# Layer-norm rows scaled by a diagonal matmul at the stage edges of a fused two-block kernel, and bias rows loaded in six parts

## The reference

```python
# first block, per layer l (c_act = silu(c); sh, sc, gt are six vectors of width 1024)
    ada = c_act @ w_ada[l] + b_ada[l]
    u = x * (1.0 + sc1) + sh1
    y = mixer(u, ...)                      # w_in (4608 columns), attention, conv, w_out
    x = layer_norm(DN_ALPHA * x + (1.0 + gt1) * y, ln_mix_g[l], ln_mix_b[l])
    u = x * (1.0 + sc2) + sh2
    h = square(relu(u @ w_up[l])) @ w_down[l]
    x = layer_norm(DN_ALPHA * x + (1.0 + gt2) * h, ln_ffn_g[l], ln_ffn_b[l])
# second block, per layer
    proj = rmsnorm(x, ln_mix_g[l]) @ w_in[l]          # 4128 columns
    # three attentions; two add a bias per head, a function of the distance of query and key
    qc = rmsnorm(cq, mla_q_norm_g[l]) @ w_uq[l]       # its last columns are rotated (rope)
```

## Time and profile before

| | us |
|---|---|
| median of 3 runs | 1823.41 |
| the profiled execution | 1823.75 |
| its span in the trace | 1822.0 |
| PE busy | 1758.1 (96%) |
| DVE busy | 1275.3 (70%) |
| ACT busy | 890.5 (49%) |

### The profile page before, as it was taken

The page is one execution under the profiler, slowest core; times in us unless marked ns, Lnnn a source line. Parts: engine busy times, 40 slices in busy tenths (PEclk is TensorE's granted clock), DMA queues, the critical chain, the costliest instruction groups (busy, mean ns, idle before and its releaser), DMA issues.

```text
span 1822.0 us, 27283 instructions
## 1 busy us (share of the span) xinstructions
PE 1758.1 (96%) x9254; PEld 1451.1 (80%) x9254; DVE 1275.3 (70%) x1973; ACT 890.5 (49%) x1530; POOL 54.8 (3%) x111
## 2 busy tenths in 40 slices
PE   8999999998999999999999999999999999999998
PEld 3776778996766789988898877788789989778886
DVE  5788897667788885568547887555555579865555
ACT  1456334443455444444556664444445557544443
POOL 0000010000000000001000000000000000000000
PEclk9999999999999999999999999999999999999999
DMA  8866568764765566653665434555546644345553
GB/s 299 266 214 220 163 219 298 254 229 138 256 219 197 196 210 209 209 188 115 204 217 155 135 121 150 185 182 187 177 145 201 208 129 159 117 151 185 185 186 125
DMA packets 215955, 346.22 MB, mean 190 GB/s; under 512 B 19531, under 2 KB 113273, under 8 KB 215593
## 3 DMA queue, kind: packets, MB, share of 16 engines
q1 hardware_dynamic: 213368, 338.89, 57.7%
q0 software_dynamic: 1632, 5.39, 0.9%
q10 hardware_dynamic: 850, 0.54, 0.1%
HBM read 343.69 MB, written 1.07 MB: 189 GB/s over the span
## 4 chain that ended last, share of the span: by engine, by line
issue 80%; PE 12%; DVE 4%; DVEq 1%; POOLq 1%; POOL 1%; ACT 0%; DMA 0%; SPq 0%; ACTq 0%
PE acc L150 2%; PE acc L148 2%; PE acc L149 2%; PE prod L223 1%; PE prod L225 1%; PE prod L224 1%; DVE w_lo L134 1%; DVEq L937 1%; PE prod L148 1%; DVE proj L938 1%; PE prod L149 1%; PE prod L150 1%; PE turn L262 0%; DVE x_res L938 0%; DVE x_res L936 0%
## 5 line engine op out<-in xcount | busy, mean ns | idle before, releaser
L134 DVE TENSOR_TENSOR w_lo<-w_raw,w_hi 128x1024 fp32r<-128x1024 f32 (+2 forms) x584 | 643.4, 1122 | 313.5 <-ACT w_hi L128 307.9
L128 ACT CAST w_hi<-w_raw 128x1024 fp32r<-128x1024 f32 (+2 forms) x584 | 557.8, 968 | 410.0 <-PE acc L150 181.6
L148 PE MATMUL prod<-w_hi,hT_hi 128*128 128x344 f32 (+2 forms) x912 | 330.5, 362 | 5.6 <-ACT proj_b L1946 5.5
L150 PE MATMUL prod<-w_hi,hT_lo 128*128 128x344 f32 (+2 forms) x912 | 323.2, 354 | 0.0
L149 PE MATMUL prod<-w_lo,hT_hi 128*128 128x344 f32 (+2 forms) x912 | 322.4, 354 | 0.0
L148 PEld LDWEIGHTS prod<-w_hi,hT_hi 128*128 128x128 f32 x912 | 172.3, 189 | 27.8 <-DVE gates L2200 4.8
L150 PEld LDWEIGHTS prod<-w_hi,hT_lo 128*128 128x128 f32 x912 | 172.2, 189 | 15.4
L149 PEld LDWEIGHTS prod<-w_lo,hT_hi 128*128 128x128 f32 x912 | 172.7, 189 | 14.5
L223 PE MATMUL prod<-uT_hi,w_hi 128*128 128x256 f32 x448 | 127.1, 284 | 1.4 <-DVE w_lo L134 0.9
L148 PE MATMUL prod<-w_hi,uT_hi 128*128 128x512 f32 x304 | 124.6, 410 | 2.7 <-DVE uT_lo L301 1.3
L224 PE MATMUL prod<-uT_lo,w_hi 128*128 128x256 f32 x448 | 126.4, 282 | 0.0
(11 more groups left out here) (349 smaller groups left out, 2785.4 us busy)
## 6 DMA issues: line engine op xcount, KB each, us to landing
w_raw<-in_w_in_dram SPq DMA_DIRECT2D x72, 512.0 KB, 3.9
ada_raw<-in_w_ada_dram SPq DMA_DIRECT2D x68, 512.0 KB, 6.8
w_raw<-in_w_in_dram SPq DMA_DIRECT2D x192, 172.0 KB, 2.4
w_raw<-in_w_up_dram SPq DMA_DIRECT2D x64, 512.0 KB, 4.3
w_raw<-in_w_down_dram SPq DMA_DIRECT2D x64, 512.0 KB, 4.7
w_raw<-in_w_gate_dram SPq DMA_DIRECT2D x128, 192.0 KB, 2.7
w_raw<-in_w_ffn_gate_dram SPq DMA_DIRECT2D x88, 256.0 KB, 3.5
w_raw<-in_w_ffn_up_dram SPq DMA_DIRECT2D x88, 256.0 KB, 4.2
```

Source lines behind the costliest of these rows:

```text
L128: act.copy(self.hi[:, s, 0:cols], self.raw[:, s, 0:cols]).then_inc(self.hi_done, 1)
L134: dve.tensor_tensor(self.lo[:, s, 0:cols], self.raw[:, s, 0:cols], self.hi[:, s, 0:cols].bitcast(F32), ALU.subtract).then_inc(self.lo_done, 1)
L148: pe.matmul(out, a_hi, w_hi, start=first and c == 0, stop=False)
L150: mm = pe.matmul(out, a_lo, w_hi, start=False, stop=last and c == chunks - 1)
```

## The change

1. At the three edges, DVE writes only `(x - mean) * g` (`centred`), which waits for the mean and not for `rstd`, and a 128x128 diagonal of `rstd` (`scale_diag`). PE lays the shift row into the bank (`lift`: four float32 matmuls with one row) and adds the rows times the diagonal (`turn_onto`: four float32 matmuls in place of the transposes). Lifts 0 and 1 stand between the products of `tok` 0 and `tok` 1 ahead of the edge, lifts 2 and 3 ahead of their turns. `edge_tile` takes the place of `turned_tile`, without fillers, and orders the products anew: hi x hi first, low weights of the last three groups at the end. DVE's and ACT's orders are changed with it; at the second edge as at the others.
2. The bias rows are loaded in six DMAs, each ahead of the loads of one tile from the sixth on, and reversed and taken in six parts behind those tiles. The small rope of `KR` moves two tiles back.
3. `rope_q` stands inside the last `branch_a`, behind one `split_lo`.
4. In layer 1 of the second block the second tile's `split_hi` stand ahead of the wait for `x_rstd`, and the tiles use `first_banks` as in layer 0. Loops over tiles are written out.

```diff
@@ -205,6 +205,63 @@
+    def edge_tile(self, pe, pos, lhs, width, outs, turn, taken, vacant, halved):
+        def products(tok, g, a, b, first=False, last=False):
+            s = (pos + g).slot(RING)
+            for c in range(KG):
+                rows = lhs[a][:, KG * g + c, tok * P:(tok + 1) * P]
+                w = (self.hi, self.lo)[b][:, s, c * width:(c + 1) * width]
+                mm = pe.matmul(outs[tok], rows, w, start=first and c == 0, stop=last and c == KG - 1)
+            return mm
+        def high(tok, g):
+            if tok == 0:
+                pe.wait_ge(self.hi_done, (pos + g).count(1 + self.groups))
+            products(tok, g, 0, 0, first=g == 0)
+        def rows_low(tok, h):
+            taken(2 * tok + h)
+            for g in (2 * h, 2 * h + 1):
+                products(tok, g, 1, 0)
+        def weight_low(tok, g):
+            if tok == 0:
+                pe.wait_ge(self.lo_done, (pos + g).count(RING + 1 + self.groups))
+            mm = products(tok, g, 0, 1, last=g == 3)
+            if tok == 0 and g == 3:
+                mm.then_inc(self.tile0_done, 1)
+            if tok == 1:
+                mm.then_inc(self.used, 1)
+        turn(0)
+        turn(1)
+        for tok in range(TOKS):
+            vacant(tok)
+            halved(2 * tok)
+            high(tok, 0)
+            high(tok, 1)
+            if tok == 0:
+                weight_low(0, 0)
+                rows_low(0, 0)
+                turn(2)
+            else:
+                rows_low(1, 0)
+                weight_low(1, 0)
+            halved(2 * tok + 1)
+            high(tok, 2)
+            high(tok, 3)
+            if tok == 0:
+                rows_low(0, 1)
+                turn(3)
+        weight_low(0, 1)
+        weight_low(1, 1)
+        rows_low(1, 1)
+        weight_low(0, 2)
+        weight_low(1, 2)
+        weight_low(0, 3)
+        weight_low(1, 3)
...
+        t.then_inc(self.full, 1)
+    def lift(self, pe, pos, rows, ones):
+        b = pos.slot(2)
+        pe.wait_ge(self.free[b], pos.over(2).count(1 + self.turns // 2))
+        for c, row in enumerate(rows):
+            pe.matmul(self.bank[b][:, c * P:(c + 1) * P], row, ones, start=c == 0, stop=False, skip_group_check=True)
+    def turn_onto(self, pe, pos, parts, scales):
+        for c, src in enumerate(parts):
+            t = pe.matmul(self.bank[pos.slot(2)][:, c * P:(c + 1) * P], src, scales, start=False, stop=c == len(parts) - 1,
+                          skip_group_check=True)
...
                     take_u_hi(3)
                 else:
-                    split(layer(l, 0, G1))
-                    for n in range(4):
+                    split(layer(l, 0, G1), 3)
+                    take_u_hi(0)
+                    split(layer(l, 3, G1), 1)
+                    for n in range(1, 4):
                         take_u_hi(n)
                 def part_take(m):
...
+            def scale_diag(tok, n):
+                dve.wait_ge(ln_rstd, n)
+                dve.tensor_scalar(rstd_diag[:, tok, :], ident, rstd[:, tok:tok + 1], None, ALU.mult).then_inc(diag_ready, 1)
+            def centred(out, rows, tok, g, done):
+                dve.scalar_tensor_tensor(out, rows, mv[:, tok, 0:1], g, ALU.subtract, ALU.mult).then_inc(done, 1)
             def normed(out, rows, tok, g, b):
...
                     if h == 0:
-                        dve.wait_ge(ln_rstd, layer(l, tok, 2 * TOKS).count(1))
-                    normed(u2_rows[:, tok, cols], x_res[:, tok, cols], tok, scale[:, cols], shift[:, cols]).then_inc(u2_ready, 1)
+                        dve.wait_ge(ln_stats, layer(l, tok, 2 * TOKS).count(1))
+                    centred(u2_rows[:, tok, cols], x_res[:, tok, cols], tok, scale[:, cols], u2_ready)
+                def u2_diag(tok):
...
                 mix_residual(0, 1)
+                next_u2(0, 0)
                 split(layer(l, at + 8, G1), 1)
+                u2_diag(0)
+                next_u2(0, 1)
                 mix_residual(1, 0)
-                next_u2(0, 0)
-                next_u2(0, 1)
                 take_u2_lo(0)
                 mix_residual(1, 1)
-                split(layer(l, at + 9, G1), 2)
                 take_u2_lo(1)
                 next_u2(1, 0)
-                split(layer(l, at + 11, G1), 1)
+                next_u2(1, 1)
+                u2_diag(1)
                 take_u2_lo(2)
-                next_u2(1, 1)
+                split(layer(l, at + 9, G1), 1)
                 take_u2_lo(3)
+                split(layer(l, at + 10, G1), 2)
                 at += G_SQ
...
                 def u_turn(n):
+                    if l > 0 and n >= 2:
+                        lift_rows(layer(l, F_U + n, F_ALL), ada_first[0:1, 0, :], n % 2)
                     pe.wait_ge(u_ready, layer(l, n, 4).count(1))
-                    rows_turn(layer(l, F_U + n, F_ALL), u_rows[:, n // 2, :], 4 * (n % 2))
-
-                W.turned_tile(pe, layer(l, 0, G1), uT, NT, outs, u_turn,
-                              lambda n: T.taken(pe, layer(l, F_U + n, F_ALL)), vacated(layer(l, 0, N_TILES)),
-                              lambda n, k: T.awake(pe, layer(l, F_U + n, F_ALL), k), 0 if l == 0 else 4, 3,
-                              lambda n: T.halved(pe, layer(l, S_U + n, S_ALL)))
+                    if l == 0:
+                        rows_turn(layer(l, F_U + n, F_ALL), u_rows[:, n // 2, :], 4 * (n % 2))
+                    else:
+                        pe.wait_ge(diag_ready, layer(2 * l - 1, n // 2, TOKS).count(1))
+                        turn_scaled(layer(l, F_U + n, F_ALL), u_rows, n)
+                u_taken = lambda n: T.taken(pe, layer(l, F_U + n, F_ALL))
+                u_halved = lambda n: T.halved(pe, layer(l, S_U + n, S_ALL))
+                if l == 0:
...
+                        pe.wait_ge(shift_ready, 2 * l + 1)
+                        for n in range(2):
+                            lift_rows(layer(l, F_U2 + n, F_ALL), ada_rest[0:1, 1, :], n)
                 def u2_turn(n):
+                    if n >= 2:
+                        lift_rows(layer(l, F_U2 + n, F_ALL), ada_rest[0:1, 1, :], n % 2)
                     pe.wait_ge(u2_ready, layer(l, n, 4).count(1))
-                    rows_turn(layer(l, F_U2 + n, F_ALL), u2_rows[:, n // 2, :], 4 * (n % 2))
+                    pe.wait_ge(diag_ready, layer(2 * l, n // 2, TOKS).count(1))
+                    turn_scaled(layer(l, F_U2 + n, F_ALL), u2_rows, n)
...
                     sp.wait_ge(bias_rows.in_dram, 16)
-                    sp.dma_start(bias_flipped, bass.AP(tensor=scratch.tensor, offset=0,
-                                                       ap=[[1, P], [REL, AH + BH], [1, SEQ]])).then_inc(bias_in, 16)
                 sp.dma_start(lat_g[:, 0:QR], row("mla_q_norm_g", QR)).then_inc(vec_in, 16)
                 sp.dma_start(lat_g[:, QR:QR + KVR], row("mla_kv_norm_g", KVR)).then_inc(vec_in, 16)
                 for n, name in enumerate(("lambda_q1", "lambda_q2", "lambda_k1", "lambda_k2")):
                     sp.dma_start(lam_vec[:, n, :], row(name, HD)).then_inc(vec_in, 16)
                 sp.dma_start(lam_const[:, :], dr["lam_const"][ls, :].to_broadcast([P, 2])).then_inc(vec_in, 16)
                 sp.dma_start(sub_g[:, :], row("diff_subln_g", 2 * HD)).then_inc(vec_in, 16)
-                with sp.Fori(1, IN2_T - LAT_TILES) as t:
-                    in_tile(t, Pos(4 * LAT_TILES, (l, G2), (t, 4)))
+                for t in range(1, IN2_T - LAT_TILES):
+                    if l == 0 and t <= BIAS_PARTS:
+                        b = t - 1
+                        sp.dma_start(bias_flipped[:, 2 * b:2 * b + 2, :],
+                                     bass.AP(tensor=scratch.tensor, offset=2 * b * REL, ap=[[1, P], [REL, 2], [1, SEQ]])).then_inc(bias_in, 16)
+                    in_tile(t, layer(l, 4 * (LAT_TILES + t), G2))
                 sp.dma_start(gates[:, 0, :], row("b_gate", 3 * D)).then_inc(late_in, 16)
                 sp.dma_start(ffn_g[:, :], row("ln_ffn_g", D)).then_inc(late_in, 16)
                 for t in range(2):
...
                         square_x(2 * l, tok)
+                    split(layer(l, 4, G2), 4, KG * IN2_W)
                 act.wait_ge(x_rstd_done, layer(l, TOKS - 1, 2 * TOKS).count(1))
...
                         H.norm(dve, n, h)
-                    split(nxt, 3, KG * GW)
+                    if last:
+                        split(nxt, 1, KG * GW)
+                        for tok in range(TOKS):
+                            taken_tiles(dve, tok, layer(l, N2_UKV + 1, N2), 2)
+                        rope_q()
+                        split(nxt + 1, 2, KG * GW)
+                    else:
+                        split(nxt, 3, KG * GW)
                     add_gate_bias(gate_tile(l, k, *per(1)), nxt + (-1), slice(t * GW, (t + 1) * GW) if last else bass.ds(t * GW, GW))
                     H.out_lo_part(dve, n, row(aT[1], t), row(aT[0], t))
                     if not last:
@@ -2331,9 +2461,6 @@
```

(11 more changed lines are left out.)

129 lines of the change are left out of this document (75 added, 54 removed).

## The result

The changed kernel took 1829.74 us (median of 7 runs, 1827.02 to 1833.38), the kernel before 1823.9 (7 runs, 1822.89 to 1825.93). The ratio is 1.0026, 95% interval 1.0015 to 1.0036: slower by 2.7 to 6.6 us, where 7 us less was forecast and 1822.0 was the upper end of the range. The profiled execution (span 1831.6) is the slowest of its seven, 3.6 above their median, so its trace holds somewhat more than the median has.

A forecast was written before the change was run, and what follows sets the result against it. TensorE, busy for 96% of the span, was taken as the bound. Terms 3.4 − 3.6 − 4.8 − 2.0 = −7.0 took the profiled 1823.75 to 1816.75, less 0.34 for the median: 1816.4 us, range 1811.8 to 1822.0.

The forecast's parts named there:

- part 1: The three edges: dearer lifts and turns, partly hidden by the new order, cost +0.8, +0.9 and +1.7, together +3.4 us.
- The replay of DVE: First edge, DVE's work stepped through in the new order: PE waits 1.9 us at turn 2.
- the bound of 0.44: Edges: upper estimate in us for one lift or turn matmul, taken as 0.22; at 0.44 they add 21 us.
- The old wait behind the first edge: PE's 0.9 us wait for a `w_lo` soon after the first edge, to be used up by the later start.
- Rival D: At the three edges the clock falls, without fillers and with 1.9 us idle: +4.2, 1820.6 us; chance 0.14.
- Part 2: Bias rows: sixth tile's weights come earlier, stall shrinks (−2.4) and the clock stays up (−1.2): −3.6 us.
- the wait of 0.9 at the sixth tile: Second block: PE's stall for the sixth tile forecast at 0.9 us in place of 3.34.
- Rival C: Sixth tile's weights stay late, other loads holding SP's queue up: −1.0 instead of −3.6, 1819.0 us; chance 0.12.
- Part 3: Moving `rope_q`: the 2.42 waits at two heads go, 0.7 each given back; layer 1's clock stays up: −4.8 us.
- Part 4: Start of layer 1: earlier `split_hi` and other banks remove PE's idle time: −2.0 us.
- the wait of 2.00: PE's idle time at the start of layer 1 in the kernel before, 2.00 us, forecast to go.
- Rival E: Edges: one-row or accumulating float32 matmuls dearer than 0.22; from 0.11 more each, over 0.2% slower; chance 0.07.

The follow-up runs named there:

- e1: The change without its edges part, edges as in the kernel before: 1811.31 us, ratio 0.9932 to the kernel before.
- e15: The whole change with lifts multiplying 128 equal rows of the shift by the identity: 1818.51 us, ratio 0.9973 to the kernel before.
- e10: The change with 128-row lifts, late `w_lo` early, seven fillers ahead of lift 2, gains and `lam_vec` work later: 1817.42 us, ratio 0.9963 to the kernel before.
- e2: Only the edges part of the change, on the kernel before: 1840.06 us, ratio 1.0082.
- e4: The change with seven filler matmuls ahead of lift 2 at each edge: 1824.68 us, ratio 0.9998 to the kernel before.
- e5: The change with the identity for both operands of the lifts, so another result: 1819.79 us, ratio 0.9969 to the kernel before.
- e8: The change's lifts and diagonal turns, but with fillers and the old order at the edges: 1824.75 us, ratio 1.0001 to the kernel before.
- e6: The change with VectorE's late `w_lo` put into its idle time at all three edges: 1828.70 us, ratio 1.0022 to the kernel before.
- e13: Only the bias rows in six parts, with the small rope moved, on the kernel before: 1821.68 us, ratio 0.9991.
- e3: Only the `rope_q` move and the new start of layer 1, on the kernel before: 1814.70 us, ratio 0.9943.
- e12: The kernel before without fillers: 1824.99 us, ratio 1.0006 to the kernel before.
- e9: e1 with layer 0's gains loaded behind the sixth tile's weights and `lam_vec` used behind the seventh's: 1808.35 us, ratio 0.9917 to the kernel before.

## Why the prediction was wrong

- **The step that failed is part 1, the edges: +3.4 forecast, +17.1 measured** (e1 against the change). The replay of DVE was right: turn 2 waits for the diagonal, 1.61 against 1.9, and the bound of 0.44 for a matmul was not needed; lifts took 0.25 to 0.27 and turns 0.22. With 128-row lifts (e15) the edges cost 7.5, still twice the forecast, and its trace against before's splits that. The first and third edge take 1.8 and 1.9 where 1.7 and 1.7 was forecast, so the replay of PE, DVE and ACT was right where the clock held: from the first lift to the next tile e15 takes 254.53 − 227.52 = 27.01 us, against 26.9. The second takes 2.9 for 0.9, with a fall of the clock in it, and 1.3 more is lost up to the third tile behind it, where PE waits 1.42 for ACT, and ACT for weights. The old wait behind the first edge, which was to absorb 0.9, absorbed 0.25. With fillers as well (e10) no edge has a fall, and in its trace they cost 2.8, 2.3 and 2.8, the fillers' overrun included. The prediction says of the kernel before that PE "waited little" there, yet each old edge has waits of 1.35 and 0.63 us; the sum does not hang on it, since it compares the starts of the next tile.
- **Rival D is the greater part of what happened**, at 0.14. It was priced at 1.4 an edge and tied to the missing fillers and the idle time of 1.9. The idle time is a part of the cause. A lift has one row, and one row at work does not hold the clock up: lift 2 and the wait behind it together let it fall, and lifts 0 and 1 can do so without any wait (e2, e4). Fillers mend the first (e4, −5.1), 128 rows mend both but for the second edge (e5 −10.4, e15 −9.7). A fall is also dearer than D had it, since behind turn 2 the new order has no wait that takes it up: the first edge costs 4.2 in the change and 1.8 in e15. I had weighed the one row for what it costs in time only, and found that rows do not matter. Even there one row is the dearer, by 0.5 an edge (e15). Loads of the stationary operand by themselves took 181 to 187 ns with one row (the change) and 187 to 192 with 128 (e15); the rule of the Trainium skill (TensorE: Matmul & The Clock Gate, LDWEIGHTS (loading the stationary operand)) stood.
- **Order against matmuls.** The forecast had the new order hide most of the matmuls' price. Where the clock mostly holds it does hide some: 12.6 in the old order (e8), 7.5 in the new (e15, with other lifts than e8). With one-row lifts it gives this back and more.
- **The slots of `w_raw`** given back late behind the second edge were not in the forecast's sum. They show as 2.57 and a fall of the clock in the profiled run, but e6 puts their price in the median below what these runs can tell. e2 has the same order and no such wait, so it comes in some executions only.
- **Part 2, −3.6 forecast**: −1.6 in e13, 2.0 or 3.4 between e1 and e3, and in the traces −1.4 (e1), −1.9 (e13) and +0.5 (the change). The mechanism was half wrong: the wait of 0.9 at the sixth tile did not come, it is 4.14, 2.98 and 2.59 in three traces. Rival C was right about this: the gains are still ahead, and the weights behind them land after 5.5 us in place of 2.4. What is gained, as I read it, is that the reversal no longer stands where it did. The size stays open between 0 and 3.5.
- **Part 3, −4.8** is 5.3 in the change's trace and 4.7 in those of e1 and e3, with 0.5 and 0.4 given back behind the two heads in the change against 0.7 each. **Part 4, −2.0**, is 3.3: the wait of 2.00 is gone, and the rest comes at the tiles behind it, whose loop is written out in the change; what of that does it was not tried. Both mechanisms are as forecast. e3 has 10.4 (7.8 to 12.8) for the two, and the 8.0 to 8.6 of the traces lies in that interval.
- Rival E, dear matmuls, was wrong in its mechanism though its sign came: slower by 4.7, with lifts at 0.25 and not at 0.33.

## What to carry to other kernels

A filler, or any small matmul that stands where the clock may fall, should use all 128 rows: the same sum with 128 equal rows, which lay in SBUF already, and the identity gave 10 us back, 1.4 of them because those matmuls are themselves a little faster. How many rows would be enough no run tells. When a transpose is replaced by a dearer matmul, first price the matmuls in the old order, then the order; here neither of the two orders paid for them, and the best version (e1, 0.9932, or e9, 0.9917, which the runs do not tell apart) leaves the edges alone. Ask of a fall of the clock, or of any slower stretch, which wait comes next: if PE waits there anyway, it costs little (e12). A wait for weights that is moved from one tile to the next, or to another queue, is still the same wait when bytes are what is late.
